# Gating the weight loads for the next layer's modulation and for the output projection on the end of each scan step's level part

## What is computed

```
mod = silu(cond) @ w_mod + b_mod            # w_mod: 1024 x 6144 per layer
u = h * (1 + sc1) + sh1
proj = u @ w_in                             # 1024 x 2432
a_out = scan over time, 6 heads, 2 directions:
    sa = S @ (-kk_t)
    S  = S * w_t + sa (x) (kk_t * a_t) + v_t (x) k_t
    y  = S @ r_t
m = concat(a_out, attention, pooling) @ w_out   # 1024 x 1024
h = layer_norm(ALPHA * h + g1 * m)
f = hier_moe(h * (1 + sc2) + sh2)           # 4 groups of 4 experts
h = layer_norm(ALPHA * h + g2 * f)
```

## Time and profile before

| | us |
|---|---|
| median of three runs | 1242.95 |
| lowest, highest | 1238.37, 1243.23 |
| profiled execution, span from first to last instruction | 1246.4 |
| three scan steps of layer 0 (214.4 to 390.2) | 175.8 |
| three scan steps of layer 1 (828.4 to 946.3) | 117.9 |

### The profile page before, as it was taken

How to read it: one execution, slowest core, us unless ns; L and a number is a source line. 1 busy time by engine, 2 the same in 40 slices (tenths; PEclk the granted TensorE clock), 3 DMA queues, 4 the chain that set the end, 5 groups by cost and what they waited for, 6 DMA issues and landing times. The chain is left out here.

```text
span 1246.4 us, 28507 instructions
## 1 busy us (share of the span) xinstructions
PE 1045.4 (84%) x12514; PEld 629.3 (50%) x12514; DVE 488.8 (39%) x1406; ACT 337.8 (27%) x751; POOL 88.0 (7%) x116
## 2 busy tenths in 40 slices
PE   3799997878777967999948999878888967999944
PEld 3466655666665533333325555567675533333333
DVE  0103856242525262322126049646645262322133
ACT  2031125332321051212114320544440051212114
POOL 1200000000000000111130000000000001111100
PEclk9899998988888987999968999889997987999977
DMA  9787543617164432899765133100005423899731
GB/s 359 271 225 280 193 176 130 226 49 271 27 188 156 158 143 97 301 382 372 260 208 149 51 104 92 46 2 4 4 10 203 141 113 94 296 373 373 263 126 51
DMA packets 145240, 217.04 MB, mean 174 GB/s; under 512 B 20691, under 2 KB 104896, under 8 KB 144672
## 3 DMA queue, kind: packets, MB, share of 16 engines
q1 hardware_dynamic: 133888, 185.61, 43.9%
q0 software_dynamic: 9088, 21.97, 4.8%
q10 hardware_dynamic: 2128, 7.47, 1.5%
HBM read 209.65 MB, written 21.10 MB: 185 GB/s over the span
## 5 line engine op out<-in xcount | busy, mean ns | idle before, releaser
L1417 ACT ACTIVATE region<-bank 128x512 f32<-128x512 f32 (+3 forms) x328 | 158.2, 513 | 277.2 <-PE bank L1324 83.0
L1298 PE MATMUL bank<-region 128*32 128x512 f32 x1152 | 174.4, 612 | 1.9 <-ACT region L1417 1.8
L1069 PE MATMUL bank<-u,ring 128*128 128x384 f32 x320 | 106.5, 488 | 0.0
L1298 PEld LDWEIGHTS bank<-region 128*32 128x32 f32 x1152 | 47.0, 112 | 109.9 <-issue 109.9
L1210 PE MATMUL bank<-u,ring 128*128 128x384 f32 x256 | 86.5, 500 | 5.9 <-DVE u L2112 5.9
L1324 PE MATMUL bank<-ring,region 128*32 128x512 f32 x768 | 87.3, 595 | 1.4 <-ACT region L1417 1.4
L2030 DVE COPY_PREDICATED region<-lev,bank 128x256 f32<-128x256 uint8 x90 | 34.8, 442 | 125.9 <-PE bank L899 125.9
L1069 PEld LDWEIGHTS bank<-u,ring 128*128 128x128 f32 x320 | 59.9, 190 | 40.7 <-issue 1.4
L1476 ACT ACTIVATE region<-bank 128x384 f32<-128x384 f32 x50 | 23.7, 491 | 184.4 <-PE bank L1069 95.6
L1210 PEld LDWEIGHTS bank<-u,ring 128*128 128x128 f32 x256 | 50.0, 196 | 41.4 <-DVE u L2112 6.3
L2237 DVE TENSOR_TENSOR region<-region,bank 128x256 f32<-128x256 f32 x24 | 10.1, 421 | 142.3 <-ACT region L1715 142.3
(11 more groups left out here) (282 smaller groups left out, 1567.9 us busy)
## 6 DMA issues: line engine op xcount, KB each, us to landing
ring<-in_w_mod SPq DMA_DIRECT2D x48, 1024.0 KB
region<-in_moe_w SPq DMA_DIRECT2D x48, 1024.0 KB
ring<-in_moe_w SPq DMA_DIRECT2D x48, 1024.0 KB
ring<-in_w_in SPq DMA_DIRECT2D x20, 768.0 KB
region<-y_rows SPq DMA_DIRECT2D x6, 1024.0 KB, 9.1
ring<-in_w_in SPq DMA_DIRECT2D x12, 256.0 KB
u_rows<-region ACTq DMA_DIRECT2D x6, 512.0 KB, 2.6
region<-in_bands POOLq DMA_DIRECT2D x2, 1280.0 KB, 7.0
```

What stands on the lines that cost most here:

```text
L1069: last = pe.matmul(dst[:, 0:T], w[:, c, tc(m)], u[:, c, :], start=(c == 0), stop=(c == KT - 1))
L1298: last = pe.matmul(bank[p % 2][cols, :], xs[:, p % 2, c, cols], of[(p * P + CTILE * q) // CAP][:, c, :], start=(c == 0), stop=(c == KT - 1))
L1417: return act.activation(dst, src, ACT.Copy)
```

## The change

Two waits are added to SP's queue. Of the 12 modulation items of layer 1, those with i = 4, 5, 6 wait until `lv_cp` is 3 (step 0's level products are copied), and those with i = 8, 9, 10 until it is 6. Items 3, 7 and 11 keep their condition, and so do 0, 1 and 2. The three output-projection items of layer 0 wait until it is 9. Nothing else changes.

```diff
@@ -537,6 +537,10 @@
                     sp.wait_ge(*used(PREV_OF[n]))
                 if kind in ("w13", "w2") and SLOT_OF[n] >= RING and i < EPG:
                     sp.wait_ge(gn_c, NT * l + 2)
+                if kind == "mod" and l > 0 and i >= 4 and i % 4 < 3:
+                    sp.wait_ge(lv_cp, NJ * (3 * (l - 1) + i // 4))
+                if kind == "out" and l + 1 < DEPTH:
+                    sp.wait_ge(lv_cp, NJ * 3 * (l + 1))
                 w = slot_view(n)
                 landed = slot_in[SLOT_OF[n]]
```

## The result

| | before | after |
|---|---|---|
| median (lowest to highest) of eight runs each, us | 1241.24 (1236.12 to 1247.82) | 1232.34 (1228.78 to 1236.32) |
| profiled span, us | 1246.4 | 1230.6 |
| three scan steps of layer 0, us | 175.8 | 159.6 |

The ratio on record is 0.9913, 95% interval 0.9888 to 0.9938, a saving of 0.9%; the two medians alone stand 8.9 us or 0.7% apart. The forecast was 1234. In the pair of profiled executions the difference is larger, 15.8 us of span, and the 16.2 us that the three steps lose are all of it. The runs after took 1.9 to 2.1 us longer than their own spans, so the profiled execution before was one of about 1248.4 us (an estimate), slower than any of the eight in the table; that one pair overstates the gain.

What follows compares the result with a forecast made beforehand. PE was taken to bound the kernel, with stops for late instruction blocks in layer 0's level parts. -19 + 7.5 + 2.5 = -9 us gave 1237.4 on the profiled span, 1234 on the median; range 1226 to 1246.

Steps and rivals of the forecast that it cites:

- The mechanism: Layer 0's level parts: PE stops when its next 256-instruction block is held behind a weight load; 18.9 us of stops.
- Rival (c): Stops are not fetches behind loads, or the moved loads do not matter; 1243 us (1240 to 1246), chance 0.06.
- Part 1: Layer 0's level parts: issue stops fall from 18.9 to 5.5 us, the first load's stop staying; gain 13.4 us.
- Part 2: Layer 0's level parts: less time at half clock after stops that go; gain 5.5 us, between 2 and 8.
- Part 3: Layer 0's chain parts: moved loads cost 7.5 us in stops (3 to 14) plus 2.5 in half clock (0 to 4).
- Part 4: SP's in-order queue and the users of its data: held loads land in time, no new wait, price 0.
- The sum: Whole kernel: level gain of 19 us less chain costs of 7.5 and 2.5 gives -9 us.
- Rival (a): Chain parts: moved loads cost there what they cost in the levels, 13 to 20 us back; 1243 us, chance 0.24.
- Rival (b): Chain parts: a fetch waits for all 6 MB queued, 30 us lost against 19 gained; 1254 us, chance 0.10.
- The figures to be seen: Layer 0's scan steps: level parts 34 to 36, 34 to 37, 32 to 34 us, clock 0.9 or more, chains 18 to 22.

Runs made afterwards that it cites:

- e4: Kernel before, with modulation items 3 to 11 and layer 0's output items bringing 64 KB per transfer; total not to be read, layer 0's scan steps 142.4 us.
- e5: Kernel before, plus one 2 MB copy within device memory in each scan step of layer 1; 1253.40 us against 1245.34.
- e3: Kernel before, nothing held; modulation items from 3 on in 0.5 MB pieces, one at a time, output items likewise; 1225.24 us, ratio 0.9852.
- e2: Kernel before, with only layer 0's three output items held; 1238.63 us, ratio 0.9969.
- e7: Changed kernel with its loads also in pieces: items 3, 7, 11 in four, held modulation items in two, output items in four; 1239.25 us, ratio 0.9968.
- e10: Kernel before, nothing held, loads in pieces of 0.25 MB with two under way; 1235.05 us, ratio 0.9913.
- e6: Kernel before, with modulation items 3 to 11 in rows of 1 KB instead of 2 KB, same bytes; 1246.19 us against 1245.34, ratio 1.0013.

## Point by point: what held, and which terms were mis-sized

**The mechanism held.** PE stops at blocks of 256 instructions whose fetch stands behind a load: e4 takes the bytes away and the stops go, e5 adds bytes and they come, e3 keeps bytes and place and shortens what is queued, and they go (in its repeat 3.9 us of small ones stay). Rival (c) is refuted by these three.

**Part 1, stops that leave the levels: right.** 18.9 less 4.9 us is 14.0, against 13.4 predicted; one stop is left for each step, with 4.9 us against 5.5. One reading beside it was not exact: in the levels one load is not always over before the next is issued. SyncE issued one at 228.68, while the one before still flowed.

**Part 2, the clock: the right size, for this pair of profiles.** From the tables, half-clock time in the level parts (twice the length times one less PEclk) fell from 36.3 us to 4.7 + 9.0 + 6.6 = 20.3. A third of the 16 us is 5.3, against 5.5. Stops and clock make 19.3 of the 20.6 us that the level parts lost; 1.3 stays unassigned. What failed is the baseline behind it: I took 20.9 us at half clock in step 1's level part to be the kernel's, and it was that execution's. In e5 the same code had a clock of 0.95 there, 3.8 us at half clock, and a part of 37.7 us where the earlier trace rows has 41.8; in e2 it had 0.91 and 39.2.

**Part 3, what the chains pay: too high.** Predicted 10 us, measured 3.1 + 2.6 - 1.3 = 4.4. The new stops have the predicted size, 7.2 us (0.7 were there before), and so do their places, one or two to a chain. Two terms failed. The stops in part replace waits for VectorE, which I had put into the lower bound and not into the value: L958's fell from 5.2 us to 3.3. And half clock in the chains rose from 13.9 us to 15.4, worth 0.5 us where I had 2.5. Together 6.5 - 1.9 + 0.5 = 5.1, near the 4.4.

**Part 4, lateness: right.** No wait for a slot in the three steps. It is the term that holds the variants in pieces back: 10.5 us in e3, 2.3 and probably another 3.6 in e7, 5.5 and probably another 5.3 in e10.

**The sum.** -20.6 + 4.4 = -16.2 us in the profiled pair against -9 forecast, while the medians give -8.9 (and -12.4 in the later comparison with the repeat). The forecast of the median thus owes something to luck, to two errors that cancel: the chains were priced 5.6 us too high, and the gain was read from an execution of before that had more half clock than others. With e5's layer 0 as the baseline the levels gain 116.2 - 101.4 = 14.8 us, where I had 19, and the chains lose 58.2 - 52.7 = 5.5, where I had 10; in all 9.3 us. That baseline is a single execution too.

**Rival (a)** would have had as much in the chains as left the levels: 13 to 20 us back against 4.4 measured. **Rival (b)** would have held a block until all 6 MB were gone: the block at 262.9 to 264.1 passes in mid-flow, and the longest chain stop is 2.3 us, far from the 10 of the rival. The reading of the earlier trace rows was right.

**The figures to be seen.** Level parts 33.6, 34.6, 33.2 (34 to 36, 34 to 37, 32 to 34), the first a little below; the clock 0.93, 0.87, 0.90, where 0.9 or more was wanted, missed in step 1; chains 20.1, 22.0 and 16.1 (18 to 22), the last below.

## What to carry to other kernels

An idle gap of about 2 us "<- issue" in a dense run of PE instructions, at a multiple of 256 of the engine's own records from the next such gap, was a late block of instructions here: look at what the DMA queues hold at that moment. One that stands off that grid (e10's 5.3 us) is something else. Put large loads where PE waits anyway, or issue them in pieces small enough that little is queued ahead of a block, but count the time that a piece costs, since late data gives the gain back (e7, e10). And before a stretch's clock is priced, look at it in a second execution of the same code.

## What was new about the hardware

- The hold does not grow with the backlog. PE entered a block at 259.16, when over 4 MB of the 6 were still to come, and its next packet started 3.8 us later; behind the loads of the level parts before, each of 2 MB or less, the packets of the nine stops started 2.6 to 4.7 us after the entry, counted by records. Without loads, in the level parts of layer 1 of the kernel before (blocks counted from e5's stops), they start 0 to 1.4 us after it, mostly 0.4 to 0.8, and take 0.9 to 1.3 us. The stops of both kernels end 1.3 to 1.6 us after their packet. An undisturbed fetch is thus about 3 us, an estimate from these three figures.
- Traffic that stays within device memory holds the fetch as well (e5), and halving the rows at equal bytes changed neither stops nor time (e6, ratio 1.0013).
- Issuing is not free when transfers pile up: the first four transfers took SyncE 0.37 to 0.70 us each, the fifth and sixth 2.64 and 3.08.
- The granted clock of one and the same stretch of code was 0.75 in one execution and 0.95 in another, 20.9 against 3.8 us at half clock; no run here shows what decides it.
